# Order of the half-array matmuls, and of some work around them, in a one-core decoder step

## What is computed

```python
h = rms_norm(x, ln_w); proj = h @ w_in                    # 1024 -> 8720 columns
# three groups of 8 heads of 64: windows 128, 512, 2048 with dilations 1, 4, 16
s = einsum('bnqhd,bnkhd->bnhqk', qb, kk)                  # own block of 128 keys and the previous one
p = exp(s - max(s)); o = einsum('bnhqk,bnkhd->bnqhd', p / sum(p), vv)
o_attn = combine_groups(outs, lses)                       # softmax over the three groups
# gated linear attention, 4 heads, 64 x 128 state, chunks of 64 tokens
new_state = exp(b_last) * state + einsum('bhsk,bhsv->bhkv', kd, v)
y = x + (sigmoid(mg_a) * ya + sigmoid(mg_b) * yb) @ w_out # ya, yb: the two gated branches, projected
```

## Time and profile before

| | |
|---|---|
| median of 3 runs | 2587.78 us (2585.11 to 2588.72) |
| the profiled execution | 2588.72 us |
| its span, first to last instruction | 2586.9 us |
| instructions | 35758, of which 13212 are MATMUL records |
| TensorE, mean granted clock | 0.992 of full speed |
| VectorE, ScalarE busy | 48%, 34% |
| chain that ended last | TensorE 95%, DMA 3% |

### The profile page before, as it was taken

The page is one execution under the profiler, slowest core; times in us unless marked ns, Lnnn a source line. Parts: engine busy times, 40 slices in busy tenths (PEclk is TensorE's granted clock), DMA queues, the critical chain, the costliest instruction groups (busy, mean ns, idle before and its releaser), DMA issues.

```text
span 2586.9 us, 35758 instructions
## 1 busy us (share of the span) xinstructions
PE 2542.8 (98%) x13212; PEld 2053.8 (79%) x13212; DVE 1242.6 (48%) x2922; ACT 890.3 (34%) x2069; POOL 197.1 (8%) x360
## 2 busy tenths in 40 slices
PE   9999999999999999999999999999999978999998
PEld 6888887887777888888888888888777734888887
DVE  5323323234331126565665665556666435655653
ACT  5224424433332224223444444445333322212211
POOL 0000000000000000121111111222122000000000
PEclk9999999999999999999999999999999988999999
DMA  5333233232332223467666655876676589433441
GB/s 185 102 125 109 93 110 105 91 95 88 105 108 84 96 80 134 145 191 227 215 209 213 198 179 185 246 252 210 198 212 194 179 289 342 187 141 124 167 163 65
DMA packets 204604, 416.63 MB, mean 161 GB/s; under 512 B 32032, under 2 KB 45808, under 8 KB 202320
## 3 DMA queue, kind: packets, MB, share of 16 engines
q1 hardware_dynamic: 163040, 295.43, 34.1%
q0 software_dynamic: 29072, 92.96, 12.8%
q10 hardware_dynamic: 12320, 25.96, 2.6%
HBM read 313.07 MB, written 112.99 MB: 165 GB/s over the span
## 4 chain that ended last, share of the span: by engine, by line
PE 95%; DMA 3%; DVE 1%; ACT 1%; issue 0%; SPq 0%; DVEq 0%; ACTq 0%
PE b_acc L1209 19%; PE b_acc L1211 19%; PE b_acc L1210 19%; PE c_p_o L1282 5%; PE c_p_s L1260 4%; PE c_p_t L1270 3%; PE f_p_b L1869 2%; PE f_p_b L1871 2%; PE f_p_b L1870 2%; PE c_p_qk L1247 2%; PE f_p_z L1869 2%; PE f_p_z L1871 2%; PE f_p_z L1870 2%; PE b_acc L1215 1%; PE b_acc L1216 1%; DMA e_vc_a<-in_cache_kv_w 1%
## 5 line engine op out<-in xcount | busy, mean ns | idle before, releaser
L1209 PE MATMUL b_acc<-b_whi,hT_hi 128*128 128x512 f32 x2048 | 822.4, 402 | 3.4 <-DVE b_wlo L942 2.1
L1211 PE MATMUL b_acc<-b_whi,hT_lo 128*128 128x512 f32 x2048 | 801.8, 391 | 0.0
L1210 PE MATMUL b_acc<-b_wlo,hT_hi 128*128 128x512 f32 x2048 | 800.4, 391 | 0.0
L1209 PEld LDWEIGHTS b_acc<-b_whi,hT_hi 128*128 128x128 f32 x2048 | 385.6, 188 | 95.2 <-issue 14.8
L1211 PEld LDWEIGHTS b_acc<-b_whi,hT_lo 128*128 128x128 f32 x2048 | 385.3, 188 | 82.8
L1210 PEld LDWEIGHTS b_acc<-b_wlo,hT_hi 128*128 128x128 f32 x2048 | 386.2, 189 | 72.6
L942 DVE SCALAR_TENSOR_TENSOR b_wlo<-b_raw,a_lnw,b_whi 128x512 fp32r<-128x512 f32 x268 | 192.8, 748 | 296.4 <-ACT b_whi L747 296.0
L1027 DVE CUSTOM_DVE_ANT_0 c_sm<-c_p_s,c_mask 128x256 f32<-128x256 f32 (+1 forms) x384 | 125.6, 363 | 370.1 <-PE c_p_s L1260 369.4
L761 ACT COPY b_stage<-b_acc 128x512 f32<-128x512 f32 (+2 forms) x198 | 115.4, 583 | 468.0 <-PE b_acc L1211 454.8
L785 ACT ACTIVATE c_sm<-c_sm,c_og 128x256 f32<-128x256 f32 (+1 forms) x384 | 174.5, 457 | 83.0 <-DVE c_og L1027 82.7
L747 ACT ACTIVATE b_whi<-b_raw,a_lnw 128x512 fp32r<-128x512 f32 x268 | 183.7, 715 | 6.1 <-PE b_acc L1211 3.5
(11 more groups left out here) (304 smaller groups left out, 3088.1 us busy)
## 6 DMA issues: line engine op xcount, KB each, us to landing
b_raw<-in_w_in SPq DMA_DIRECT2D x134, 512.0 KB, 4.4
tm<-b_stage SPq DMA_DIRECT2D x256, 256.0 KB, 2.2
a_x<-tm POOLq DMA_DIRECT2D x192, 256.0 KB, 4.5
b_ck<-in_cache_kv_w POOLq DMA_DIRECT2D x104, 256.0 KB, 4.7
c_qk<-tm SPq DMA_DIRECT2D x101, 256.0 KB, 4.1
f_m<-tm SPq DMA_DIRECT2D x16, 1024.0 KB, 5.7
c_v<-tm SPq DMA_DIRECT2D x53, 256.0 KB, 4.3
og<-c_og ACTq DMA_DIRECT2D x48, 264.0 KB, 3.9
```

Source lines behind the costliest of these rows:

```text
L1209: nc.tensor.matmul(out, stat_hi, mov_hi, start=(k == 0), stop=False)
L1210: nc.tensor.matmul(out, stat_hi, mov_lo, start=False, stop=False)
L1211: return nc.tensor.matmul(out, stat_lo, mov_hi, start=False, stop=(k == KC - 1))
```

## The change

It has five edits.

1. `scores`: the loop over the halves `h` goes outside that over the blocks, so a far unit runs both matmuls of head 0 and then both of head 1.
2. `outer`: the loop over chunks goes outside; the wait for the earlier state is split, so that chunk 0 waits only for the step that it needs.
3. `pv` takes one batch `b` instead of four units of both batches: it runs all units of batch 0, and a second call those of batch 1. It waits for each buffer when it comes to it and releases each when it is read. `v_slot` and `load_v` number the buffers of group 2 by batch first. The calls for groups 0 and 1 become two each; for pair 2, `pv(2, 1, 1)` comes after `gla_outer(3)`.
4. ScalarE, tile 8: `low_branches` comes after `scale_ol(t + 2)` instead of before it.
5. VectorE, tile 8: `mix(t)` comes before `split_lo1(t + 1)`, as for the other tiles.

```diff
@@ scores
-                    for n in blocks:
-                        b = 1 if n == x.i else 0
-                        for h in range(2):
-                            r = slice(HD * h, HD * h + HD)
+                    for h in range(2):
+                        r = slice(HD * h, HD * h + HD)
+                        for n in blocks:
+                            b = 1 if n == x.i else 0
@@ outer
-                    if n >= 1:
-                        pe.wait_ge(st_done, 2 * n)
-                    for a in range(NP):
-                        cols = slice(2 * GV_W * a, 2 * GV_W * (a + 1))
-                        for c in range(2):
-                            t = slice(CHUNK * c, CHUNK * c + CHUNK)
+                    for c in range(2):
+                        t = slice(CHUNK * c, CHUNK * c + CHUNK)
+                        if n >= 1:
+                            pe.wait_ge(st_done, 2 * (n - 1) + c + 1)
+                        for a in range(NP):
+                            cols = slice(2 * GV_W * a, 2 * GV_W * (a + 1))
                             last = nc.tensor.matmul(pt[:, c, cols], kdT[t, a, :], gv[t, n % 2, cols], start=True, stop=True)
-                            if a == NP - 1:
-                                last.then_inc(u_done, 1)
+                        last.then_inc(u_done, 1)
@@ v_slot
-    return V_PER_PAIR * n + (0 if g == 0 else 1 + b if g == 1 else 3 + b + 2 * (c // 4))
+    return V_PER_PAIR * n + (0 if g == 0 else 1 + b if g == 1 else 3 + 2 * b + c // 4)
@@ load_v
-                c, b = divmod(r - 3, 2)
+                b, c = divmod(r - 3, 2)
@@ pv
-        def pv(n, g, part):
-            k, units = n % 2, range(4 * part, min(4 * part + 4, UNITS[g]))
-            for b in range(2):
-                w = v_slot(n, g, b, units[0])
-                pe.wait_ge(vc_in[w % VSLOTS], 16 * (w // VSLOTS) + 16)
-            for c in units:
-                for b in range(2):
-                    w = v_slot(n, g, b, c)
-                    stat = pm0[:, k, 64 * b:64 * b + 64] if g == 0 else (pm1, pm2)[g - 1][:, k, b, 64 * c:64 * c + 64]
-                    last = nc.tensor.matmul(p_o[64 * b:64 * b + 64, k, :], stat, vc(w)[:, b if g == 0 else c % 4, :],
-                                            start=False, stop=(g == 2 and c == UNITS[g] - 1))
-                    if c == units[-1] and (g or b):
+        def pv(n, g, b):
+            k, seen = n % 2, -1
+            for c in range(UNITS[g]):
+                w = v_slot(n, g, b, c)
+                if w != seen:
+                    if seen >= 0:
                         last.then_inc(v_used, 1)
+                    pe.wait_ge(vc_in[w % VSLOTS], 16 * (w // VSLOTS) + 16)
+                    seen = w
+                stat = pm0[:, k, 64 * b:64 * b + 64] if g == 0 else (pm1, pm2)[g - 1][:, k, b, 64 * c:64 * c + 64]
+                last = nc.tensor.matmul(p_o[64 * b:64 * b + 64, k, :], stat, vc(w)[:, b if g == 0 else c % 4, :],
+                                        start=False, stop=(g == 2 and c == UNITS[g] - 1))
+            if g or b:
+                last.then_inc(v_used, 1)
@@ main of the tensor part, pair 2
             pv(2, 0, 0)
+            pv(2, 0, 1)
             pv(2, 1, 0)
             gla_outer(2)
             gla_outer(3)
+            pv(2, 1, 1)
@@ main of the scalar part
-                if t == SAMPLE_AT:
-                    low_branches(t)
...
                 if t + 2 < TILES:
                     scale_ol(t + 2)
+                if t == SAMPLE_AT:
+                    low_branches(t)
@@ main of the vector part
-                if t == SAMPLE_AT:
-                    split_lo1(t + 1)
                 mix(t)
-                if t + 1 < TILES and t != SAMPLE_AT:
+                if t + 1 < TILES:
                     split_lo1(t + 1)
```

More of the change, by code:

```diff
@@ L1934, in main @@
             pv(0, 0, 0)
+            pv(0, 0, 1)
             pv(0, 1, 0)
+            pv(0, 1, 1)
             gla_turn()
@@ L1942, in main @@
             pv(1, 0, 0)
+            pv(1, 0, 1)
             pv(1, 1, 0)
+            pv(1, 1, 1)
             gla_within()
@@ L1965, in main @@
             pv(3, 0, 0)
+            pv(3, 0, 1)
             pv(3, 1, 0)
+            pv(3, 1, 1)
             pv(3, 2, 0)
```

## The result

The kernel after takes 2603.73 us (median of 4 runs, 2601.39 to 2604.19), beside 2587.23 us for the kernel before (4 runs, 2585.11 to 2588.72): a ratio of 1.0062, 95% interval 1.0045 to 1.008. It is 16.5 us slower; 49 had been forecast. The direction was right and the size was not: 2603.7 lies inside the stated range, far under the forecast's own one (2626 to 2649), and 2.7 us from rival (a), 2601. The profiled execution of after took 2602.14 us, span 2600.4, so 13.5 us more span than before. Each of the two profiled executions lies some 1.5 us from its median, towards the other; the traces are therefore compared with each other, and account for 13.5. The runs of after go with their granted clock: the two at 0.997 took 2601.39 and 2602.14 us, the three at 0.995 and 0.996 took 2603.43 to 2604.19; the profiled one is of the first kind.

A forecast was written before the change was run, and what follows sets the result against it. TensorE was taken as the bound, busy 98% of the span, with waits only in the sample's attention and last part. 24.2 + 6.9 + 9.1 + 9.1 = +49.3 us gave 2638.0, stated as 2637 us; range 2598 to 2662.

The forecast's parts named there:

- the forecast's own one: Narrower range of whole-kernel time, 2626 to 2649 us, allowing new load waits in the sample's attention or a cheaper tile 8.
- rival (a): Array pairs past blocked matmuls: `scores` and `outer` cost 0, `pv` 88 steps, about +4, tile 8 added: 2601 us; chance 0.17.
- matmuls start in program order: TensorE: a matmul waiting for its half blocks everything behind it; basis for pairs lost in `scores`, `outer` and `pv`.
- Edit 1, +24.2 forecast: `scores`: six steps of a pass instead of four per far unit, 0.224 us each over 108 units.
- Edit 2, +6.9 forecast: `outer`: two more steps of 0.216 us in each of 16 tiles; bounds 0 and 13.8.
- chunk 0's earlier release: `outer`: worth nothing, since TensorE doesn't wait there.
- Edit 3, +9.1 forecast: `pv`: 97 steps against 52, +38.7 us, less 23.5 of waits and 10 of slow clock, plus 4; bounds +5, +20.
- 4 us of two waits: Sample's attention: the part of the waits for buffers landing near 2103.7 and at 2112.0 that isn't recovered.
- other loads on SyncE's queue: Sample's attention: these delayed the 7.39 us wait's buffer, issued at 2091.59, so it still lands near 2103.7.
- Edits 4 and 5, +9.1 forecast: Tile 8: a longer ScalarE and VectorE chain leaves TensorE idle 7.5 us, plus 1.6 of slow clock; bounds +6, +11.
- (b): Rival: no pair at all forms where a half changes, in `scores`, `outer` and `pv`; 2674 us, chance 0.12.
- (d): Rival: pairing survives everywhere and single-buffer release ends the attention's waits, about -25, tile 8 +9: 2572 us; chance 0.03.

The follow-up runs named there:

- m1_halves: Bare kernel replacing the whole kernel: k matmuls on one array half, then k on the other; k = 3 at 512 columns took 3.70 us.
- pv_four: Kernel before with the two loops of `pv` swapped inside a call, four matmuls of batch 0 then four of batch 1: 2589.84 us, ratio 1.0008.
- state_late: Kernel before with the four loads of the recurrent states issued two buffers later on SyncE's queue: 2588.75 us, ratio 1.0005.
- loads_late: Kernel before with the four recurrent state loads two buffers later and six loads of the branches' weights later too: 2586.38 us, ratio 0.9998.
- pv_only: Kernel before with only the `pv` change (one batch per call, buffers waited for and released singly): 2592.29 us, ratio 1.002.
- t8_undone: Kernel after with both tile 8 reorderings (ScalarE's `low_branches`, VectorE's `mix`) undone: 2593.45 us, ratio to before 1.0025.

## Why the prediction was wrong

**The step that failed** is "matmuls start in program order: a matmul waits for its half, and what stands behind it waits too". It carried 31.1 of the 49.3 us (edits 1 and 2), which measured nothing that can be told from 0, and the count of edit 3. The rows of m1_halves, of after at 2075.93 and of pv_four at 2079.60 all show a matmul of the free half starting past up to three waiting passes. A far unit of `scores` and a product of `outer` have just two matmuls per half, within reach, so every pair survives. The prediction had read from the earlier trace rows that the second matmul overtakes the first one's second pass, and called it a unit kept in order; it was the visible end of a reach that the alternating order could not show further. It gave this a chance of 0.17 as rival (a), with the mechanism and 2601 us. That rival's number came close partly by luck: its 88 steps, put through the prediction's own sum, give 31.0 - 23.5 - 10 + 4 = +1.5 us, not the "about +4" that it states.

The Trainium skill ("TensorE: Matmul & The Clock Gate", Part 3, what overlaps) says that matmuls are strictly first in, first out, without reordering; it is weight loads that it has pulled ahead. For matmuls in different halves of the array no trace here agrees: with k = 3 at 512 columns strict order gives 10 steps, 4.5 us, and 3.70 was measured; at 2075.93 a later matmul starts ahead of three earlier passes. No row shows one half's own passes out of order.

**Edit 1, +24.2 forecast:** 0. A far unit takes 0.72 us as before; the second half's first pass starts 13 ns behind the first instead of 7, which over 108 units is 0.65 of the 0.7 us between 1570.7 and 1571.4.

**Edit 2, +6.9 forecast:** 0; 1.14 us as before. That chunk 0's earlier release is worth nothing was right.

**Edit 3, +9.1 forecast:** +6.0 in its stage by the trace, +4.6 by time alone. Its shape was right: pairs go, waits go, the slow clock goes. The steps are 92, not 97 (34.4 us, not 38.7), since calls of groups 0 and 1 still pair across their border; a wait of 3.6 us stays, where 4 us of two waits was allowed; the slow clock gave 8.5 where 10 was estimated: 10.2 was lost to it before, but 1.7 is still lost behind the wait that stays. The prediction's own arithmetic has two slips, neither of which matters: its terms add up to 9.2, and by its rule the last pair has 23 steps and not 24, since nothing stands between its groups 1 and 2. Rival (a) had 88 steps: it took those calls to pair entirely, and they reach two matmuls far.

That the 7.39 us wait ended when it did because of "other loads on SyncE's queue" was right for this one wait and wrong as a limit of the stage. The buffer is issued late for that reason, but with another order the next buffer is waited for instead (state_late, loads_late). In after this stage had one wait, until 2100.76, and none for the buffer that landed at 2103.7 before.

**Edits 4 and 5, +9.1 forecast:** 7.34 + 2.0 = 9.3. Right in the chain, in the wait (7.5 foretold) and in the slow clock (1.6). The 1.6 us of slow clock at tile 0 went away besides, in after and in pv_only, which wasn't forecast; the wait there is 0.3 us shorter. In t8_undone, with edit 3 too, the clock fell behind a wait of 2.90 us, so it can't be counted on as a gain of the edit. What decides it, no run here takes apart.

The accounts close: -0.1 + 6.0 - 0.3 + 5.8 + 2.0 = +13.4 us for 13.5 of span. The 16.5 between the medians are 3 us more; the 1.6 us of tile 0, which t8_undone paid and the profiled execution of after did not, may be part of them. Of the rivals, (b) and (d) fall with m1_halves: pairs do form at a change of half, and only two float32 matmuls deep.

## What to carry to other kernels

If matmuls use half of the array, look at how many passes of one half stand in a row: float32 can be grouped by twos and one-pass types by fours at no cost here, and beyond that every further matmul runs alone. Before trusting that an engine keeps an order, look for a row in which it breaks it, and measure how far, with a sequence longer than the kernel has: it takes one small kernel. Don't put a short instruction on which the bounding engine waits behind one that waits for a load; and price an idle TensorE with its slow clock behind it (7.3 us of wait cost 9.3). Before a microsecond or two is put down to an edit, look at the granted clock behind short waits in both traces: it may have fallen in one and not in the other.

## What was unexpected in the hardware

- TensorE starts matmuls of a free half past up to three waiting passes of the other half, for halves of the rows and of the columns, float32 and fp32r (3.70 us for three float32 matmuls of 512 columns on each half, 0.75 for four one-pass ones of 256).
- A lone pass costs as much as a pair: 0.11 us at 128 columns, 0.43 at 512, so eight float32 matmuls of 512 columns on one half take 7.08 us, and eight on each half in runs of eight 12.29.
- The length of a short wait doesn't tell the granted clock behind it. At tile 0 it fell after 2.90 us (t8_undone, transposes 1.94 us) and not after 2.96 and 3.04 us (pv_only, after, 1.06 us); the same wait of 2.2 us near 1826 us was followed by a fall in five traces of eleven.
- Issuing two 1 MB loads 8 us earlier left the total of the waits for such loads at 24.1 us against 23.5.
